# A two-layer hybrid decoder step: the up-projections of two merged branches as three products of rounded and low parts

## The reference, cut to what matters

```python
h = rms_norm(x, lp['norm_g']) * (1.0 + scale[:, None]) + shift[:, None]
proj = jnp.einsum('btd,de->bte', h, lp['w_in'])
...
# each branch output o is (tokens, 256) and gated by its own SiLU; then, for the four branches n
merged = sum(sigmoid(gate_columns[n]) * (o[n] @ w_up[n]))      # w_up[n]: 256 x 1024
x = x + gate * (merged @ w_out)
```

## Time and profile before

| what | value |
|---|---|
| median of 3 runs | 1532.18 us (1531.87 to 1536.23) |
| profiled execution | 1531.77 us, its span 1530.0 us |
| TensorE busy | 1417.8 us, 93% of the span |
| VectorE, ScalarE, GpSimd busy | 42%, 34%, 31% |
| granted TensorE clock, mean | 0.972 of full speed |

### The profile page before, as it was taken

One profiled execution on the slowest core, in us unless ns is written; L12 is line 12 of the kernel. 1 busy time (PEld: TensorE's weight loads), 2 busy tenths in 40 slices (PEclk: granted clock), 3 DMA queues, 4 the chain that ended last, 5 costly groups with the idle time before them and its releaser, 6 DMA issues.

```text
span 1530.0 us, 33517 instructions
## 1 busy us (share of the span) xinstructions
PE 1417.8 (93%) x14880; PEld 1283.5 (84%) x14880; DVE 641.9 (42%) x1115; ACT 517.6 (34%) x780; POOL 473.3 (31%) x350
## 2 busy tenths in 40 slices
PE   6799999999999999897979999999899999989896
PEld 4698999989899888775879898999888988878695
DVE  5756412417322336535133861132444242663522
ACT  5533422224422244143433252221542223514322
POOL 0244522123312122157723452122322122312620
PEclk9899999999999999998999999999999999999998
DMA  9532231225321354476543323122263126246811
GB/s 318 181 97 70 73 91 45 58 57 110 109 76 51 64 107 121 102 261 212 166 127 83 94 70 84 44 51 63 70 142 83 44 57 120 76 121 174 272 42 56
DMA packets 275908, 162.18 MB, mean 106 GB/s; under 512 B 86102, under 2 KB 244922, under 8 KB 275252
## 3 DMA queue, kind: packets, MB, share of 16 engines
q1 hardware_dynamic: 274100, 159.06, 38.1%
q10 hardware_dynamic: 1664, 0.98, 0.2%
HBM read 135.25 MB, written 24.89 MB: 105 GB/s over the span
## 4 chain that ended last, share of the span: by engine, by line
PE 75%; DVE 13%; ACT 5%; issue 3%; DMA 2%; ACTq 1%; SPq 1%; POOL 0%; DVEq 0%
PE psA L836 31%; PE psA L844 15%; PE psA L886 6%; PE psB L772 3%; PE psB L781 3%; PE psB L782 2%; PE psB L717 2%; DVE RA L1946 1%; PE psB L959 1%; DVE small_rows L1837 1%; DMA RB<-in_ada_w 1%; PE psB L969 1%; PE psB L1402 1%; ACT w_hi L1436 1%; DVE small_rows L1838 1%
## 5 line engine op out<-in xcount | busy, mean ns | idle before, releaser
L708 POOL TENSOR_TENSOR w_lo<-ring,w_hi 128x512 fp32r<-128x512 f32 x274 | 381.7, 1415 | 941.7 <-ACT w_hi L1436 881.0
L836 PE MATMUL psA<-h_hi,w_hi 128*128 128x260 f32 x1984 | 428.9, 298 | 23.2 <-DVE h_lo L1852 12.8
L836 PE MATMUL psA<-h_lo,w_hi 128*128 128x260 f32 x1984 | 404.2, 286 | 0.0
L836 PEld LDWEIGHTS psA<-h_hi,w_hi 128*128 128x128 f32 x1984 | 310.5, 191 | 41.8 <-issue 19.9
L836 PEld LDWEIGHTS psA<-h_lo,w_hi 128*128 128x128 f32 x1984 | 310.8, 191 | 0.2
L844 PE MATMUL psA<-h_hi,w_lo 128*128 128x260 f32 x1984 | 274.5, 286 | 0.0
L844 PEld LDWEIGHTS psA<-h_hi,w_lo 128*128 128x128 f32 x1984 | 249.6, 187 | 5.3 <-issue 1.0
L1436 ACT CAST w_hi<-ring 128x1024 fp32r<-128x1024 f32 x133 | 137.2, 1033 | 32.4 <-PE psA L844 18.8
L787 ACT COPY ws<-psB 128x128 f32<-128x128 f32 x80 | 21.4, 268 | 248.6 <-PE psB L772 248.6
L795 DVE COPY_PREDICATED tg<-tmask,psB 128x128 f32<-128x128 uint8 x40 | 14.2, 356 | 133.4 <-PE psB L782 95.2
L1466 ACT ACTIVATE tg<-psA 128x520 f32<-128x520 f32 x48 | 28.8, 600 | 88.5 <-PE psA L844 88.3
(11 more groups left out here) (476 smaller groups left out, 2356.7 us busy)
## 6 DMA issues: line engine op xcount, KB each, us to landing
ring<-in_w_in SPq DMA_DIRECT2D x122, 512.0 KB, 4.2
scr_tanh<-tg SPq DMA_DIRECT2D x48, 260.0 KB, 4.6
ring<-in_ada_w SPq DMA_DIRECT2D x18, 512.0 KB, 4.4
upw<-in_w_up SPq DMA_DIRECT2D x64, 128.0 KB, 3.9
RA<-scr_tanh SPq DMA_DIRECT2D x30, 260.0 KB, 4.1
RB<-in_ada_w SPq DMA_DIRECT2D x14, 512.0 KB, 5.7
ws<-scr_tanh SPq DMA_DIRECT2D x24, 260.0 KB, 4.4
ring<-in_w_out SPq DMA_DIRECT2D x9, 512.0 KB, 4.9
```

Source lines behind the costliest of these rows:

```text
L708: nc.gpsimd.tensor_tensor(tile_part(RL[s][:, k], (kind, n)), tile_part(RS[s][:, k], (kind, n)), tile_part(HS[L.hslot[q]][:, k], (kind, n)) ...
L836: nc.tensor.matmul(out(h), HS[L.hslot[q]][:, p, 0:m], cols(part(p), h), start=(p == 0 and part is hi), stop=False)
```

## The change

The 16 `up` tiles of branches A and D are computed in parts like the gates: `up_hi` is the rounded slice of `w_up` (ScalarE, `up_split`), `up_lo` the rest (GpSimd), `out_hi` the rounded branch output (ScalarE, `out_split`), `out_lo` the rest, made by VectorE for A (inside `first_out`) and by GpSimd for D. Each is then 12 matmuls of type fp32r instead of 4 of plain fp32. The dictionaries `ups_after` and `outs_after` say after which gate's tanh ScalarE makes a rounding; the first three of A are made ahead of the copy into `mrow`. GpSimd makes the low part ahead of the low weights of the gate two places further on. The other 16 `up` tiles stay plain. To make room, `svA` shares memory with `svB`, and `cT` with `vv` and `so`. The step lists of the second layer change as those of the first.

```diff
--- before.py
+++ after.py
@@ -114,7 +114,8 @@
         ring, wlo = sb_parts("ring", "w_lo", [P, RING, KT, P])
-        upw = sb("upw", [P, RING, 2, P])
+        upw, uplo = sb_parts("upw", "up_lo", [P, RING, 2, P])
+        uphi = sb("up_hi", [P, RING, 2, P], F32R)
         whi = sb("w_hi", [P, 2, KT, P], F32R)
@@ -123,7 +124,6 @@
         G = sb("G", [P, KT, 9])
-        cT = sb("cT", [P, KT, 9])
         chl = sb("c_parts", [P, KT, 18], F32R)
@@ -140,12 +140,13 @@
         crowA = mg5[0:11, 2:4, :].rearrange("p a b -> p (a b)")[:, 0:7 * P]
-        svA = sb("svA", [P, 6, NB, 2])
         svB = sb("svB", [P, 8, NB, 2])
+        svA = svB[:, 0:6]
         rowA = prow
         vecA = vecB = sb("vec", [P, 8, HD])
-        vv = sb("vv", [P, 3, 16])
-        so = sb("so", [P, 3, 16])
+        decode_small = sb("decode_small", [P, 96])
+        vv, so = (decode_small[:, 48 * k:48 * k + 48].rearrange("p (n v) -> p n v", n=3) for k in range(2))
+        cT = decode_small[:, 0:72].rearrange("p (k s) -> p k s", k=KT)
         sa = sb("sa", [P, 2, 16])
@@ -229,7 +230,7 @@
                     "pe_c", "act_c", "dve_c", "pe_s", "act_s", "dve_s", "pe_p", "act_p", "act_w", "pool_w",
-                    "pe_n", "act_n", "dve_n", "pe_m", "act_m", "dve_m")}
+                    "act_u", "pool_u", "pe_n", "act_n", "dve_n", "pe_m", "act_m", "dve_m")}
                 self.n_ada = 24 if n == 0 else 8
@@ -474,6 +475,13 @@
                 return 2 if b in (1, 3) else 1
+
+            pu = TR["pool_u"]
+            out_f = (RA[:, 2:4, :], RD[:, 4:6, :], RC[:, 0:2, :], RB[:, 4:6, :])
+            out_hi = (wsr[:, 8:10, :], mhi[:, 6:8, :])
+            out_lo = (RAlo[:, 2:4, :], mhi[:, 4:6, :])
+            up_slot = lambda idx: idx % UP_RING
+            IN_PARTS = 16
 
@@ -699,10 +707,24 @@
 
+            ups_after = {10: (3,), 11: (4,), 12: (5,), 13: (6,), 14: (7,), 22: (8,), 23: (9,), 24: (10,), 25: (11,), 26: (12,),
+                         27: (13, 14), 28: (15,)}
+            outs_after = {9: (0,), 23: (1,)}
+            two_on = lambda g: SPLIT[SPLACE["gate", g] + 2]
+            UPS_AT = {two_on(g): idxs for g, idxs in ups_after.items()}
+            UPS_AT[two_on(8)] = (0, 1, 2)
+            OUTS_AT = {two_on(g): bs for g, bs in outs_after.items() if g != 9}
+
             @block.gpsimd
...
                     s, _ = ring_slot(kind, n, L)
+                    for idx in UPS_AT.get((kind, n), ()):
+                        pool.wait_ge(*TR["act_u"].at("uhi", idx))
+                        nc.gpsimd.tensor_tensor(uplo[:, up_slot(idx)], upw[:, up_slot(idx)], uphi[:, up_slot(idx)], sub).then_inc(*pu.step("ulo"))
+                    for b in OUTS_AT.get((kind, n), ()):
+                        pool.wait_ge(*an.at("ohi", b))
+                        nc.gpsimd.tensor_tensor(out_lo[b], out_f[b], out_hi[b], sub).then_inc(*pu.step("olo"))
                     pool.wait_ge(*aw.at("hi", q))
@@ -864,8 +886,6 @@
 
-                outs = (RA[:, 2:4, :], RB[:, 4:6, :], RC[:, 0:2, :], RD[:, 4:6, :])
-
                 def gate(idx, parts=range(PARTS)):
@@ -876,15 +896,30 @@
 
-                    if idx in (0, 8, 16, 24):
-                        pe.wait_ge(*dn.at("gated", idx // 8))
+                    b, first = idx // 8, idx % 8 == 0
+                    if first:
+                        pe.wait_ge(*(an.at("ohi", b) if idx < IN_PARTS else dn.at("gated", b)))
                     psum_free("up", idx)
-                    pe.wait_ge(L.up[idx % UP_RING], 16 * (idx // UP_RING + 1))
-                    out = psum("up", idx)
+                    if idx >= IN_PARTS:
+                        pe.wait_ge(L.up[up_slot(idx)], 16 * (idx // UP_RING + 1))
+                        out = psum("up", idx)
+                        for i in range(2):
+                            for hf in range(2):
+                                last = nc.tensor.matmul(out(hf), upw[:, up_slot(idx), i, :], out_f[b][:, i, hf * HALF:(hf + 1) * HALF], start=(i == 0), stop=(i == 1))
+                        last.then_inc(*pm.step("gate"))
+                        return
+                    pe.wait_ge(*TR["act_u"].at("uhi", idx))
+                    out, s = psum("up", idx), up_slot(idx)
+                    for x in (out_hi[b], out_lo[b]):
+                        if x is out_lo[b] and first:
+                            pe.wait_ge(*(pu.at("olo", b - 1) if b else dn.at("olo")))
+                        for i in range(2):
+                            for hf in range(2):
+                                nc.tensor.matmul(out(hf), uphi[:, s, i, :], x[:, i, hf * HALF:(hf + 1) * HALF], start=(i == 0 and x is out_hi[b]), stop=False)
+                    pe.wait_ge(*pu.at("ulo", idx))
                     for i in range(2):
                         for hf in range(2):
-                            last = nc.tensor.matmul(out(hf), upw[:, idx % UP_RING, i, :], outs[MERGE[idx][0]][:, i, hf * HALF:(hf + 1) * HALF],
-                                                    start=(i == 0), stop=(i == 1))
+                            last = nc.tensor.matmul(out(hf), uplo[:, s, i, :], out_hi[b][:, i, hf * HALF:(hf + 1) * HALF], start=False, stop=(i == 1))
                     last.then_inc(*pm.step("gate"))
@@ -934,7 +969,7 @@
                 pe.wait_ge(*da.at("prep"))
-                nc.tensor.transpose(psB[0:96, 0, 0:P], svA[:].rearrange("p n b i -> p (n b i)"), ident).then_inc(*ps_.step("rows"))
+                nc.tensor.transpose(psB[0:96, 0, 0:P], svA.rearrange("p n b i -> p (n b i)"), ident).then_inc(*ps_.step("rows"))
                 pe.wait_ge(*as_.at("rows", 0))
@@ -1452,6 +1487,18 @@
 
+                def up_split(idx):
+
+                    act.wait_ge(L.up[up_slot(idx)], 16 * (idx // UP_RING + 1))
+                    if idx >= UP_RING:
+                        act.wait_ge(*pm.at("gate", idx - UP_RING))
+                    nc.scalar.copy(uphi[:, up_slot(idx)], upw[:, up_slot(idx)]).then_inc(*TR["act_u"].step("uhi"))
+
+                def out_split(b):
+
+                    act.wait_ge(*dn.at("gated", b))
+                    nc.scalar.copy(out_hi[b], out_f[b]).then_inc(*an.step("ohi"))
+
                 def gates(*idxs):
@@ -1464,6 +1511,10 @@
                         A(half(th_tile(idx)), psA[:, b:b + 2, 0:HALF], ACT.Tanh, scale=0.5).then_inc(*am.step("th"))
+                        for b in outs_after.get(idx, ()):
+                            out_split(b)
+                        for k in ups_after.get(idx, ()):
+                            up_split(k)
                         if SPLACE["gate", idx] + 2 < SPLACE["ada", 0]:
@@ -1632,6 +1683,8 @@
                     after_fill()
+                for idx in range(3):
+                    up_split(idx)
                 act.wait_ge(*pa.at("mt"))
@@ -2084,6 +2137,8 @@
                     gated(0, outs3[0], RA[:, 7:9, :])
+                    dve.wait_ge(*an.at("ohi", 0))
+                    T_(out_lo[0], out_f[0], out_hi[0], sub).then_inc(*dn.step("olo"))
 
...
@@ -2406,9 +2461,11 @@
...
+    'act_u0': 'uhi uhi uhi uhi uhi uhi uhi uhi uhi uhi uhi uhi uhi uhi uhi uhi'.split(),
+    'pool_u0': 'ulo ulo ulo ulo ulo ulo ulo ulo ulo ulo olo ulo ulo ulo ulo ulo ulo'.split(),
...
```

More of the change, by code:

```diff
@@ L2408 @@
     'pool_w0': 'lo lo lo lo lo lo lo lo lo lo lo lo lo lo lo lo lo lo lo lo lo lo lo lo lo lo lo lo lo lo lo lo lo lo lo lo lo lo lo lo lo lo lo lo lo lo lo lo lo lo lo lo lo lo lo lo lo lo lo lo lo lo lo lo lo lo lo lo lo lo lo lo lo lo lo lo lo lo lo lo lo lo lo lo lo lo lo lo lo lo lo lo lo lo lo lo lo lo lo lo lo lo lo lo lo lo lo lo lo lo lo lo lo lo lo lo lo lo lo lo lo lo lo lo lo lo lo lo lo lo lo lo lo lo lo lo lo lo lo lo lo lo lo lo lo lo lo lo lo lo lo lo lo lo lo lo lo lo lo lo lo lo lo lo lo lo lo lo lo lo lo lo lo lo lo lo lo lo lo lo lo lo lo lo lo lo lo lo'.split(),
+    'act_u0': 'uhi uhi uhi uhi uhi uhi uhi uhi uhi uhi uhi uhi uhi uhi uhi uhi'.split(),
+    'pool_u0': 'ulo ulo ulo ulo ulo ulo ulo ulo ulo ulo olo ulo ulo ulo ulo ulo ulo'.split(),
     'pe_n0': 'mean var var var'.split(),
-    'act_n0': 'sq ln rn tz sq ln rn tz tz sq ln rn tz'.split(),
-    'dve_n0': 'cen normed gains bonus siluz gated normed siluz gated siluz gated normed siluz gated'.split(),
+    'act_n0': 'sq ln rn tz ohi sq ln rn tz ohi tz sq ln rn tz'.split(),
+    'dve_n0': 'cen normed gains bonus siluz gated olo normed siluz gated siluz gated normed siluz gated'.split(),
     'pe_m0': 'gl gl gl gl gl gl gl gl gl gl gate gl gate gl gate gl gate gl gate gl gate gl gate gate gl gl gl gl gl gl gl gl gl gate gl gate gl gate gate gl gate gate gl gate gate gl gate gate gl gl gate gate gate gate gate gate gate gate gate gate gate gate gate gate out out out out out out out out'.split(),
@@ L2436 @@
```

(6 more changed lines are left out.)

## The result

The changed kernel takes 1551.04 us (median of 4 runs, 1544.72 to 1551.62), the kernel before 1532.62 us (4 runs beside them): a ratio of 1.0106, 95% interval 1.0075 to 1.0137. Measured once more later (e5), the ratio was 1.0070 (1.0046 to 1.0094). So it is slower, by 12 to 18 us where +6 was forecast. The profiled execution took 1551.62 us.

The account below looks back on a forecast made before the run. The prediction took the kernel as bound by a chain three quarters TensorE, with ScalarE and VectorE latencies paid in full. Terms +1.9, +5.0, -0.7 and +0.2 gave +6.4, taken as 6.2: 1538.2 us, range 1533.5 to 1543.

Parts of the forecast that it names:

- (b): Rival: longer gaps at `up(0)` drop TensorE's clock; with VectorE blocked and `up(4)`'s load late, 1543 us; chance 0.13.
- the forecast's 0.60: Chance given to the main forecast, a time of 1535.5 to 1541.5 us for the whole kernel.
- VectorE's delay by the `ulo`: GpSimd's low-part weight subtractions 0 to 3, some 0.63 us each alone, overlap VectorE's convolution, adding about 0.25 us.
- The product: An up-projection in parts takes 12 matmuls, 1.45 us against 1.56 plain: 0.11 us saved each, much of it lost.
- Edit 1: Three weight roundings on ScalarE ahead of `mrow` lengthen the head-sum wait: 0.95 us per layer, 1.9 in all.
- Edit 2: Making branch A's output halves delays `up(0)` and VectorE's convolution: +2.9 us in layer 0, +2.1 in layer 1.
- Gate 12: Sign: it starts about 3.9 us later in layer 0, 3.1 in layer 1; under 2 us would refute the prediction.
- The load of `up(4)`: Branch A weight load lands near 386.7, before the tanh ends at about 387.5: free, with 0.8 us to spare.
- Edit 3: Branch D's roundings and low parts against quicker tiles: +0.1 us per layer (bounds -0.6 and +1.0), +0.2 in all.
- (a): Rival: the waits around the head sums and branch A's output are mostly absorbed: +3 us, 1535; chance 0.15.
- (c): Rival: each of the 32 changed up-projections saves 0.35 us, latencies cost at most 5 us: 1526 us; chance 0.05.
- (d): Rival: nothing moves, waits of 3 us against savings of 3.5 us: 1532 us; chance 0.07.

Follow-up runs that it names:

- e5: Changed kernel as it is, measured once more against the kernel before: 1545.58 us, ratio 1.0070.
- e10: Kernel before, plus two unused 128x1040 VectorE subtractions behind branch A's gated output, for which `up(0)` does not wait: 1540.27 us, ratio 1.0043.
- e2: Kernel before, plus only the three 128x256 weight roundings on ScalarE ahead of the copy into `mrow`, all `up` tiles plain: 1537.53 us, ratio 1.0031.
- e9: Kernel before, with `up(0)` made to wait for an unused ScalarE copy of branch A's gated output: 1537.44 us, ratio 1.0030.
- e4: Changed kernel with only branch D's `up` tiles in parts, branch A plain as before: 1534.63 us, ratio 0.9998.
- e1: Changed kernel plus unused matmuls in four TensorE waits per layer (head sums, ahead of and inside `up(0)`, gate 14): 1540.88 us, ratio 1.0047.
- e7: Kernel before plus unused matmuls per layer: 13 ahead of the first head sums, 17 ahead of `up(0)`, 7 ahead of gate 14: 1531.68 us, ratio 0.9972.
- e12: Kernel of e7 plus 24 unused matmuls in branch B's chunk 1 and 12 ahead of the lru products, per layer: 1528.97 us, ratio 0.9960.
- e6: Changed kernel with branch A's first three tiles plain, output halves made during `up(0)` (rounded) and after `up(2)` (low, GpSimd): 1537.42 us, ratio 1.0025.

## Why the prediction was wrong

**The direction and the mechanism of the waits were right.** The step that failed is the sum itself: it has no term for the clock. I had seen, a gap of 2.20 us with the clock fallen behind it, and put it into rival (b) with 0.13 and one fall of "1.2 us or more"; the forecast's 0.60 went to a case in which every gap grows and the clock stays. The clock's share is 5 to 9.8 of the 13.5 us that ten runs show, the rest 3.7 to 8 us, of the order of my +6.2. The second step that failed is a size, VectorE's delay by the `ulo`; it stands below. None of the three signs that I had named for a wrong prediction showed (gate 12 late by under 2 us, another pace, a wait of `up(8)` for GpSimd): none of them looked at the clock.

**The falls and their price.** It is not one fall but several: behind the head sums, behind `up(0)`, and in branch D's recurrence some 40 us later, where after is at the lower clock for 13.6 us a layer by the windows above, and before for 3.4 us in layer 0 and 6.8 in layer 1. The price of one can be read in layer 1 of before against e10, where the clock stayed up at `up(0)`:

```profile
1112.97 0.40 PE L836 MATMUL psA<-h_hi,w_hi 128*128 128x260 f32 x2
```

```profile
1115.35 2.02 PE L886 MATMUL psA<-RA,upw 128*128 128x260 f32 x8 [2.21 <-DVE RA L1925]
...
1118.16 0.40 PE L836 MATMUL psA<-h_hi,w_hi 128*128 128x260 f32 x2
```

`up(0)` of before at 1108.50 starts 6.85 us later in e10, the pair of gate matmuls at 1112.97 only 5.19 us later (1118.16): 1.66 us of TensorE's time for one stretch. How much of it arrives depends on what TensorE waits for next. Behind the head sums of after all of it does (below). Behind `up(0)` of after little can, since TensorE waits another 1.00 us ahead of gate 12, for ScalarE and through it for VectorE.

**The product.** Right: 377.67 to 379.10 is 1.43 us, forecast 1.45; the plain form takes 1.56.

**Edit 1.** The wait went from 1.63 to 2.54 us in both layers, +0.91 where I had +0.93. Alone (e2) it came to +4.3 us by the medians instead of 1.9; the table's rest is 2.1 us, and the clock makes up the difference.

**Edit 2.** The wait inside `up(0)` was 1.09 us ("near 1") and VectorE's subtraction 1.38 us in layer 0, 1.73 in layer 1 (1.4). The wait ahead of `up(0)` stayed at 2.23 us instead of 3.4: VectorE's last two instructions of branch A took 1.67 us each instead of 2.2, so the gated output came 1.1 us earlier; GpSimd was at its `ulo` just then (from 361.80), instead of a gate's low weights. (In e9, without the `ulo`, the wait is 3.29 us.) GpSimd's `ulo` were under-priced: 0.63 us each was my estimate; here are the timeline of POOL around them and the group over all 32:

```profile
363.50 3.42 POOL L724 TENSOR_TENSOR up_lo<-upw,up_hi 128x256 fp32r<-128x256 f32 x2
...
378.85 0.76 POOL L724 TENSOR_TENSOR up_lo<-upw,up_hi 128x256 fp32r<-128x256 f32 x1 [5.09 <-ACT up_hi L1495]
```

```profile
L724 POOL TENSOR_TENSOR up_lo<-upw,up_hi 128x256 fp32r<-128x256 f32 x32 | 36.2, 1138 | 170.5 <-ACT up_hi L1495 170.5
```

The median of the 32 is 0.74 us, but the first three took 1.7 us each, beside VectorE's last instructions of branch A. The Trainium skill (SBUF — State Buffer, Who interferes with whom) has the two engines' shared port as an exclusive lock. The trace agrees that each holds up the other: 1.7 for 0.74 us here, 2.2 for 1.24 us in e10's subtractions, and 3.18 us for the `ulo` at 388.47, beside one VectorE instruction of 3.41 us.

**Gate 12.** It came 388.15 - 383.71 = 4.4 us later in layer 0, but from a start 1.6 us early: TensorE's wait for the head sums begins at 340.01 in after, at 341.60 in before. So the delay to hold against my 3.9 us (edit 1 included) is 6.0 us, and 4.9 us in layer 1 against 3.1. On VectorE both layers add up alike, step by step against before: +0.9 us by edit 1, +1.7 by the fall of the clock behind the head sums, -1.1 by the quicker gated output, +2.8 by the wait for ScalarE and the subtraction (I had 2.65), and +1.7 by branch D's convolution itself. The timelines of DVE, of before and then of after, at the convolution's start and end:

```profile
366.44 5.97 DVE L2095 SCALAR_TENSOR_TENSOR ws<-RD,parT,ws 128x510 f32<-128x510 f32 x6
...
380.17 0.15 DVE L2110 COPY colbg<-cst 128x1 f32<-128x1 f32 x1
```

```profile
369.18 7.10 DVE L2150 SCALAR_TENSOR_TENSOR ws<-RD,parT,ws 128x510 f32<-128x510 f32 x6
...
384.62 0.15 DVE L2165 COPY colbg<-cst 128x1 f32<-128x1 f32 x1
```

13.7 us have become 15.4 (the same in layer 1), where I had 0.25 us for the `ulo`. What runs on GpSimd meanwhile is mostly not `ulo` but the gates' low weights, which the three `ulo` pushed back from VectorE's last instructions of branch A into the convolution. The contention moved: 1.1 us came back ahead of `up(0)`, 1.7 us were lost behind it.

The load of `up(4)` was in time, as forecast: its rounding at 388.00 follows the tanh at once.

**Edit 3.** Not contradicted: +0.2 us for both layers forecast, +0.2 us by the means of e4, though its interval of -3 to +2.5 us can't tell 0.2 from 2. Chunk 1 of branch B does wait longer there, 5.5 us instead of 3.8 in layer 0 and 4.7 instead of 3.7 in layer 1; where that comes back I did not trace.

**The rivals.** (b) named the right mechanism and too few falls, 1543; (a), (c) and (d) fell. The Trainium skill (TensorE: Matmul & The Clock Gate, HAM oscillation — how this bites in real kernels) describes a kernel in which waits let the clock fall, so that each next tile begins slowly. I did not weigh that against the trace as a rival of its own; e1, e7 and e12 bear it out in kind. What stays open is why the stretches in branch D's recurrence come and go. In after the first begins at 410.8, inside a wait of 1.27 us ahead of gate 14; before has 0.95 us there and kept the full clock in layer 0, not in layer 1. The second begins at 424.5 among small matmuls (4x512 and less), with no wait since 411.82. Both were shorter in e1, where 9 fillers stand in that very wait and the longer waits up to 70 us earlier are filled as well; no run filled this wait alone.

## What to carry to other kernels

Where TensorE is most of the chain, a wait has two prices: its length, and up to half of the stretch at the lower clock that may follow, less what the next wait hides. Read PEclk by windows behind every gap that a change lengthens; if the trace of before has one fall behind such a gap, put the fall into the sum, not into a rival. And before a product is made cheaper by 7%, count what must be ready ahead of its first tile: here the first three tiles of branch A, of 16 a layer, gave most of the loss (8 of 12 us in e6 against e5), and filling the existing gaps with unused matmuls gained more than the change could have.

## What was not expected of the hardware

A gap of 2.54 us had the clock fall behind it in one layer of e2 and not in the other, in one and the same execution; the 94 runs of before beside the experiments reach from 1528.2 to 1542.9 us, and their time follows the mean clock with a correlation of -0.88. TensorE's unused matmuls of 0.12 us, up to 24 of them in a wait, took 4.6 us off a kernel in which it was busy 93% of the span. And VectorE's convolution of branch D changes its length with what GpSimd does beside it, by 3.5 us: 13.7 us up to the copy into `colbg` in before, 15.4 in after, and 11.9 in e10, where it began later and the added instructions, 2.2 us each instead of 1.24, met GpSimd's low weights in its place. So a delay of 4.4 us arrived as 2.5.
